# Standard products leave the recurrence over chunks; score and value products are regrouped

## Time and profile before

| what | value |
|---|---|
| median of three runs | 2170.67 us (2167.99 to 2173.81) |
| the profiled execution's own time | 2169.13 us |
| its span, first to last instruction | 2167.2 us |
| TensorE busy, matmul / weight loads | 98% / 86% |
| VectorE / ScalarE / GpSimd busy | 49% / 19% / 23% |
| mean granted TensorE clock | 0.997 of full |
| L782, all standard products | 2816 records, 697.3 us |

### The profile page before, as it was taken

The page is one execution under the profiler, slowest core; times in us unless marked ns, Lnnn a source line. Parts: engine busy times, 40 slices in busy tenths (PEclk is TensorE's granted clock), DMA queues, the critical chain, the costliest instruction groups (busy, mean ns, idle before and its releaser), DMA issues.

```text
span 2167.2 us, 48810 instructions
## 1 busy us (share of the span) xinstructions
PE 2132.3 (98%) x21490; PEld 1869.5 (86%) x21490; DVE 1065.8 (49%) x1786; ACT 409.5 (19%) x1169; POOL 505.5 (23%) x377
## 2 busy tenths in 40 slices
PE   9999999999999999999999999999999999999997
PEld 8999977777887679999899999777778877799996
DVE  4554344442726624773645443444437265247745
ACT  1111122222103511110211121222221034111002
POOL 3433300002011123333224333000020111234331
PEclk9999999999999999999999999999999999999998
DMA  8544333335633365554354453222355333655551
GB/s 295 175 163 169 125 121 106 107 106 194 221 138 97 98 231 178 161 178 161 125 174 167 156 175 125 101 101 100 100 210 196 137 98 107 242 167 166 171 174 66
DMA packets 88979, 329.50 MB, mean 152 GB/s; under 512 B 11904, under 2 KB 11920, under 8 KB 86464
## 3 DMA queue, kind: packets, MB, share of 16 engines
q1 hardware_dynamic: 74592, 268.60, 36.8%
q0 software_dynamic: 11872, 53.59, 6.8%
q10 hardware_dynamic: 2304, 4.20, 0.6%
HBM read 315.91 MB, written 18.82 MB: 154 GB/s over the span
## 4 chain that ended last, share of the span: by engine, by line
PE 94%; DVE 2%; DMA 1%; ACT 1%; issue 0%; SPq 0%; POOL 0%; DVEq 0%; POOLq 0%
PE PB L782 29%; PE PB L832 3%; PE PB L850 3%; PE PB L846 3%; PE PB L841 3%; PE PB L836 3%; PE PB L823 3%; PE PB L826 3%; PE PB L1238 3%; DMA WT<-in_w_all 1%; PE PB L906 1%; PE PB L988 1%; PE PB L971 1%; PE PB L973 1%; PE PB L966 1%; PE PB L962 1%
## 5 line engine op out<-in xcount | busy, mean ns | idle before, releaser
L782 PE MATMUL PB<-XT,WT 128*128 128x264 f32 (+1 forms) x2816 | 697.3, 395 | 1.6 <-DMA WT<-in_w_all 1.6
L782 PEld LDWEIGHTS PB<-XT,WT 128*128 128x128 f32 (+1 forms) x2816 | 506.0, 189 | 107.1 <-issue 19.6
L1433 ACT ACTIVATE VT<-PB 128x132 f32<-128x132 f32 (+2 forms) x280 | 79.1, 291 | 580.1 <-PE PB L836 131.4
L617 POOL DMA_DIRECT2D out<-in_c_win x16 | 8.1, 506 | 471.2 <-DVE ARENA L1998 471.2
L1433 ACT ACTIVATE ARENA<-PB 128x128 f32<-128x128 f32 (+6 forms) x173 | 73.1, 447 | 223.8 <-PE PB L762 56.9
L617 POOL DMA_DIRECT2D ARENA<-in_c_sel x64 | 40.0, 625 | 238.5 <-issue 238.5
L638 POOL TENSOR_TENSOR TOEP<-WT 128x1024 f32<-128x1024 f32 x20 | 47.2, 2358 | 181.3 <-PE PB L836 133.8
L638 POOL TENSOR_TENSOR TOEP<-H 128x1024 f32<-128x1024 f32 x20 | 48.2, 2409 | 139.9 <-PE PB L836 135.4
L832 PE MATMUL PB<-ARENA,TOEP 128*128 128x132 f32 x640 | 78.7, 276 | 0.5 <-POOL TOEP L641 0.5
L836 PE MATMUL PB<-ARENA,TOEP 128*128 128x132 f32 x640 | 78.6, 276 | 0.0
L841 PE MATMUL PB<-ARENA,TOEP 128*128 128x132 f32 x640 | 78.6, 276 | 0.0
(11 more groups left out here) (450 smaller groups left out, 4177.5 us busy)
## 6 DMA issues: line engine op xcount, KB each, us to landing
WT<-in_w_all SPq DMA_DIRECT2D x340, 512.0 KB, 4.5
H<-in_w_all SPq DMA_DIRECT2D x120, 512.0 KB, 4.5
KNVC<-in_w_all SPq DMA_DIRECT2D x40, 512.0 KB, 3.9
out<-in_c_win POOLq DMA_DIRECT2D x16, 512.0 KB, 4.9
ARENA<-in_c_cmp POOLq DMA_DIRECT2D x64, 128.0 KB, 5.0
ARENA<-in_c_sel POOLq DMA_DIRECT2D x64, 128.0 KB, 4.8
TOEP<-in_toep POOLq DMA_DIRECT2D x2, 2048.0 KB, 8.4
ARENA<-in_states POOLq DMA_DIRECT2D x4, 1024.0 KB, 11.5
```

The lines of the kernel that those rows point to most:

```text
L782: ins = mm(PB[rows, bank, 0:T], WT[:, s, k, 0:rows.stop - rows.start], x, start=start, stop=stop)
L1433: return act(out, in_, ACT.Copy)
```

## The change

1. In the recurrence no standard product is issued behind `r`, `u` and the result products (`BEHIND` 0 in place of 1); `EARLY` falls from 21 to 18. The 48 products a layer that this frees are issued in front of the gate pairs (90 in place of 42). All other counts of the plan stay.
2. The four result products with the old state move from behind `s` to behind `r`; in front of them TensorE waits for ScalarE's copy of the chunk before (`o`).
3. A unit's score products are reordered: 256, 512, 512, then the wait, then 256.
4. The compressed values are made by 48 products with 32 weight columns, in turn for the four column groups, and lie on all 128 partitions: the samples' in bank 1 (two for each column group), the prompt's in bank 2. VectorE takes them out with two instructions over 128 partitions.
5. The samples' attention follows: the transposed compressed scores are made at four places, ScalarE copies `PCZ` in four parts for each parity, the products with compressed values use rows 32m to 32m + 14 for column group m, and the products with the new rows come first, with a step `n` that the compressed ones wait for.

```diff
-EARLY = 21
+EARLY = 18
...
-    BEHIND.update({f"r{chunk}": 1, f"u{chunk}": 1, f"s{chunk}": 1})
+    BEHIND.update({f"r{chunk}": 0, f"u{chunk}": 0, f"s{chunk}": 0})
...
                         mark("rw_t", it, ins, f"r{c}")
+                        if c:
+                            wait(("rw_a", f"o{c - 1}"))
+                        for w, cq in pairs:
+                            for ra in both:
+                                mm(PB[ra, 2, cq], ST[ra, c % 2, w, :], AR[ra, w * NCH + c, 1, :], start=False, stop=True, skip_group_check=True)
                         project(L, hq, f"r{c}")
...
                         mark("rw_t", it, ins, f"s{c}")
-                        for w, cq in pairs:
-                            for ra in both:
-                                mm(PB[ra, 2, cq], ST[ra, c % 2, w, :], AR[ra, w * NCH + c, 1, :], start=False, stop=True, skip_group_check=True)
...
-                        for s in range(NSQ):
-                            for g in range(NG):
-                                ins = mm(PB[0:NBLK, 1 + s // 2, (s % 2) * 256 + g * HD:(s % 2) * 256 + g * HD + HD],
-                                         hx[:, g // 2, s, g % 2, :], W2[:, :], start=True, stop=True)
-                    if kd:
-                        for r in range(4):
-                            for g in range(NG):
-                                ins = mm(PB[32 * r:32 * r + NBLK, 5, 256 + g * HD:256 + g * HD + HD],
-                                         hx[:, g // 2, NB, g % 2, :], W2[:, :], start=True, stop=True)
+                        blocks = lambda g, s: ARENA[:, at_hx + 135 * g + NBLK * s:at_hx + 135 * g + NBLK * s + 32]
+                        for g in range(NG):
+                            for i in range(2):
+                                for r in range(4):
+                                    ins = mm(PB[32 * r:32 * r + 32, 1, i * 256 + g * HD:i * 256 + g * HD + HD], blocks(g, 2 * r + i), W2[:, :], start=True, stop=True)
+                            for r in range(4):
+                                ins = mm(PB[32 * r:32 * r + 32, 2, g * HD:g * HD + HD], blocks(g, NB), W2[:, :], start=True, stop=True)
...
-                    for e in range(2):
-                        if e:
-                            pe.wait_ge(*step("sc_t", it, "s0"))
-                        ins = mm(PB[:, 2, e * 256:e * 256 + 256], H[half(e), Q0 + u, 0:P], keys(e)[:, :, 0:P], start=True, stop=True)
-                        if e == 0:
-                            mark("sc_t", it, ins, "s0")
-                        ins = mm(PB[:, 1 - e, :], H[half(1 - e), Q0 + u, P:SEQ], keys(1 - e)[:, :, 0:SEQ], start=True, stop=True)
+                    ins = mm(PB[:, 2, 0:256], H[half(0), Q0 + u, first], keys(0, P), start=True, stop=True)
+                    mark("sc_t", it, ins, "s0")
+                    mm(PB[:, 1, :], H[half(1), Q0 + u, second], keys(1, SEQ), start=True, stop=True)
+                    ins = mm(PB[:, 0, :], H[half(0), Q0 + u, second], keys(0, SEQ), start=True, stop=True)
+                    mark("sc_t", it, ins, "s1")
+                    pe.wait_ge(*step("sc_t", it, "s0"))
+                    ins = mm(PB[:, 2, 256:512], H[half(1), Q0 + u, first], keys(1, P), start=True, stop=True)
...
-                mark("as_t", L, transpose(PB[0:NBLK, 5, 0:P], SCS[:, 0:NBLK]), "pt")
+                for r in range(4):
+                    ins = mm(PB[32 * r:32 * r + NBLK, 5, 0:P], SCS[:, 0:NBLK], ident, start=True, stop=True)
+                mark("as_t", L, ins, "pt")
...
+                for br in range(2):
+                    for m in range(NB // 2):
+                        ins = mm(PB[32 * m:32 * m + 32, 4, 0:256], PNT[:, br, 32 * m:32 * m + 32],
+                                 VT[0:NB, 2, 2 * br * P:2 * br * P + 256], start=br == 0, stop=False)
+                mark("as_t", L, ins, "n")
...
+                    pe.wait_ge(*step("as_t", L, "n"))
                     for m in range(NB // 2):
                         b = 2 * m + odd
-                        mm(PB[32 * m:32 * m + 32, 4, 0:256], PCZ[:, b, :], VC[:, b, :], start=False, stop=False)
+                        rows = slice(32 * m, 32 * m + NBLK)
+                        ins = mm(PB[32 * m:32 * m + 32, 4, 0:256], PCZ[rows, b, :], VC[rows, odd, :], start=False, stop=odd == 1)
...
-                    copy(PCZ[:, odd:NB:2, cols], own_rows(PB[0:NBLK, 5, 0:P]))
+                    for m in range(NB // 2):
+                        rows = slice(32 * m, 32 * m + NBLK)
+                        copy(PCZ[rows, 2 * m + odd, cols], own_rows(PB[rows, 5, 0:P])[:, m])
...
-                        for r in range(4):
-                            rows = slice(32 * r, 32 * r + NBLK)
-                            stt(VCP[rows, :].rearrange("p (g d) -> p g d", d=HD), PB[rows, 5, 256:512].rearrange("p (g d) -> p g d", d=HD),
-                                0.5, spread(B2V[rows, L, :].unsqueeze(1), NBLK, NG, HD), ALU.mult, ALU.add)
-                        src = PB[0:NBLK, 1:6, :].rearrange("p a b -> p (a b)")[:, 0:NSQ * 256].rearrange("p (g d) -> p g d", d=HD)
-                        ins = stt(KNVC[0:NBLK, :].rearrange("p (g d) -> p g d", d=HD), src, 0.5,
-                                  spread(B2V[0:NBLK, L, :].unsqueeze(1), NBLK, NSQ * NG, HD), ALU.mult, ALU.add)
+                        stt(VCP.rearrange("p (g d) -> p g d", d=HD), PB[:, 2, 0:256].rearrange("p (g d) -> p g d", d=HD),
+                            0.5, spread(B2V[:, L, :].unsqueeze(1), P, NG, HD), ALU.mult, ALU.add)
+                        ins = stt(KNVC[:, 0:8 * HD].rearrange("p (g d) -> p g d", d=HD), PB[:, 1, :].rearrange("p (g d) -> p g d", d=HD), 0.5,
+                                  spread(B2V[:, L, :].unsqueeze(1), P, 2 * NG, HD), ALU.mult, ALU.add)
```

More of the change, by code:

```diff
@@ L208, in hybrid_trunk @@
         KN = KNVC[:, 0:8 * T].rearrange("p (t n) -> p t n", n=T)
-        VC = KNVC[0:NBLK, :].rearrange("p (s n) -> p s n", n=4 * HD)
+        VC = KNVC[:, 0:8 * HD].rearrange("p (i n) -> p i n", n=4 * HD)
         V1 = sb("V1", [P, 8, 32])
@@ L290, in hybrid_trunk @@
         used[0] -= 9 * T
+        at_hx = used[0]
         HX, HY, HT = take(P, 2, 270), take(P, 2, 270), take(P, 2, 270)
@@ L312, in hybrid_trunk @@
         PTZ = take(P, 4 * NB, 32).rearrange("p (i b) n -> p i b n", b=NB)
-        PCZ, PNT, OS = take(NBLK, NB, 32), take(NB, 2, P), take(P, 256)
+        PCZ, PNT, OS = take(P, NB, 32), take(NB, 2, P), take(P, 256)
         assert used[0] <= at_att
@@ L379, in hybrid_trunk @@
         steps("cb", DEPTH, t="sc pt", v="zero add max sub sum rc cg ok ps", a="exp pt")
-        steps("sc", DEPTH * UNITS, t="s0 s", v="add max", a="exp")
+        steps("sc", DEPTH * UNITS, t="s0 s1 s", v="add max", a="exp")
         steps("pv", DEPTH * UNITS, t="pt0 pt1 o", v="rc cg ps", a="pt0 pt1")
         steps("po", DEPTH * UNITS, v="o")
-        steps("as", DEPTH, t="sc0 sc1 pt o tr", a="exp pt os", v="zero q gm gsr add max rc cg ps back")
+        steps("as", DEPTH, t="sc0 sc1 pt n o tr", a="exp pt os", v="zero q gm gsr add max rc cg ps back")
         steps("zb", DEPTH, a="tanh", v="sz out")
@@ L1277, in scores @@
                     it = L * UNITS + u
-                    keys = lambda a: H[half(a), KV0 + 4 + g2:KV0 + 9 + g2:4]
-                    for e in range(2):
-                        if e:
-                            pe.wait_ge(*step("sc_t", it, "s0"))
-                        ins = mm(PB[:, 2, e * 256:e * 256 + 256], H[half(e), Q0 + u, 0:P], keys(e)[:, :, 0:P], start=True, stop=True)
-                        if e == 0:
-                            mark("sc_t", it, ins, "s0")
-                        ins = mm(PB[:, 1 - e, :], H[half(1 - e), Q0 + u, P:SEQ], keys(1 - e)[:, :, 0:SEQ], start=True, stop=True)
+                    keys = lambda a, n: H[half(a), KV0 + 4 + g2:KV0 + 9 + g2:4][:, :, 0:n]
+                    first, second = slice(0, P), slice(P, SEQ)
+                    ins = mm(PB[:, 2, 0:256], H[half(0), Q0 + u, first], keys(0, P), start=True, stop=True)
[5 more added lines that the diff above has]
+                    ins = mm(PB[:, 2, 256:512], H[half(1), Q0 + u, first], keys(1, P), start=True, stop=True)
                     mark("sc_t", it, ins, "s")
@@ L1369, in _ @@
                             mm(PB[32 * m:32 * m + 32, 4, 0:256], PTZ[:, i, 2 * m + odd, :], SVS[odd][:, m, i, :],
-                               start=odd == 0 and i == 0, stop=False)
+                               start=False, stop=False)
+                    pe.wait_ge(*step("as_t", L, "n"))
                     for m in range(NB // 2):
                         b = 2 * m + odd
-                        mm(PB[32 * m:32 * m + 32, 4, 0:256], PCZ[:, b, :], VC[:, b, :], start=False, stop=False)
-                for br in range(2):
-                    for m in range(NB // 2):
-                        ins = mm(PB[32 * m:32 * m + 32, 4, 0:256], PNT[:, br, 32 * m:32 * m + 32],
```

(3 more changed lines are left out.)

## The result

| | before | changed |
|---|---|---|
| median of the runs, us | 2171.38 (2167.99 to 2173.81, 4 runs) | 2195.2 (2191.39 to 2206.61, 4 runs) |
| ratio, 95% interval | 1 | 1.0124 (1.0103 to 1.0146) |
| profiled execution and its span, us | 2169.13, 2167.2 | 2191.39, 2189.7 |
| mean granted clock, each run | 0.997 (profiled) | 0.983, 0.987, 0.987, 0.989 |

The change makes the kernel slower by 1.2%, about 24 us. The forecast was 2176.4, its range 2170.5 to 2188.0: the time lies outside. The last line of the table holds the main cause.

A forecast was written before the change was run, and what follows sets the result against it. TensorE was taken as the bound, at 94% of the chain that ended last. Recurrence and moved products net +15.2, values -7.4, scores -4.1, sample attention +2.0: +5.7, so 2176.4 us against the median, range 2170.5 to 2188.

The forecast's parts named there:

- the fourth rival: Recurrence chunks: the clock falls once they lose their filling, +22 us more, 2198; chance 0.03.
- The recurrence's static saving: Recurrence: shorter pauses take a chunk from 3.52 to 2.66 us; over 32 chunks -27.5 us.
- The 96 moved products: Run ahead of the gates: standard products taken from the chunks cost 0.445 us each there, +42.7 us.
- Compressed values: Compressed values: four column groups stream side by side, 1.6 us in place of 5.29; -7.4 us in all.
- Scores: Score products: a unit takes 1.48 in place of 1.82 us; twelve units count, -4.1 us.
- Sample attention: Sample attention: six more copies, a change of product kind and three more products cost 1.0 us, twice: +2.0 us.
- The new waits: Waits for o in the chunks and for step n in the sample attention: passed under other work, cost nothing.
- The first rival: Recurrence: pauses don't shrink, 0.24 us is the true hand-over, a chunk of 3.23 us, 2194.6; chance 0.09.
- the second: Values and scores: packing fails, column groups and row halves run one after the other, 2187.9 us; chance 0.07.
- The sum without the recurrence: Forecast terms of values (-7.4), scores (-4.1) and sample attention (+2.0) together: -9.5 us.

The follow-up runs named there:

- e5: Changed kernel with useless filler products in the chunks' pauses, 128 columns behind r, 256 behind u and s: 2185.38 us, ratio 1.0072.
- e7: Changed kernel with the first half of the result products back behind s: 2205.07 us, ratio 1.0164.
- e2: Changed kernel with the recurrence's part undone, so all of the change but that: 2163.81 us, ratio 0.9959 against before.
- e1: Kernel before with the recurrence's part of the change alone: 2207.63 us, ratio 1.0168.
- e9: Kernel before with the new order of the scores alone: 2167.12 us, ratio 0.9977.
- e6: Kernel with all but the recurrence's part, plus six standard products of each layer moved in front of two waits: 2156.62 us, ratio 0.9927 against before.

## Why the prediction was wrong

**The step that failed is the clock's.** The forecast held it at 1.00 in the chunks and gave its fall, the fourth rival, 0.03, with the words that a chunk "would have products streaming in 1.15 of 2.66 us, and its longest gap is below 0.6". The argument took the one row with a level below 1.00, at 2.96 busy of 17 us, as if nothing between that and full work could lower it. The earlier trace rows said nothing of the range between. And its sentence that the trace shows a lower level "only at the end" is wrong. The trace of before has these windows in layer 1, ahead of a round's chunks, the first with an idle time of 1.56 us near its end:

```profile
1456.00:1459.70 3.70, 2.14 (x37) 1.58 (x38) 0.69 (x1) 0.17 (x1) 0.00 (x0) 1.00 0.03 10
1459.70:1463.10 3.40, 3.40 (x38) 2.39 (x38) 0.69 (x2) 0.22 (x1) 0.00 (x0) 0.50 0.02 5
```

So a short pause amid small products had been followed by the low level before anything was changed. Windows over the whole span, and not over three stretches, would have found it. The runs then showed more: with 7.31 us busy of 10.80 in the chunks the clock fell in four of eight rounds, in e5, with 10.4 of 10.8, in the chunks of none. The rival's price per chunk was right (0.72 measured, 0.69 forecast). Its extent was not: it took all 32 chunks, +22; in the profiled run seven or eight were hit, some in part, which cost 3 us (first r to last s takes 11.07, 10.41, 10.04 and 10.16 in the four rounds, 9.68 in the others). The rest lies in the work behind them, whose standard products stream twice as long. In all that is 7 us in the two profiled executions (against e5), and 11 to 20 by the ratios of the changed kernel (1.0124, 1.0145) and e7 (1.0164) against e5's 1.0072.

The Trainium skill, "TensorE: Matmul & The Clock Gate", A second HAM failure mode, reports a kernel whose clock swung because TensorE idled briefly and often. The traces agree: idle times of 0.35 to 0.38 in each chunk, and stretches of 7 to 10 us at the low level. The prediction named this rule and set it aside for want of a row, though its own trace had one, the two windows above.

**The recurrence's static saving** was -27.5. The chunk is right within 0.02. But e5, at a full clock, saves 24.8 against the profiled execution of before, and 673.02 - 651.37 = 21.7 against e2, which differs only in this part and the fillers. What is missing is about 1 us of a low stretch at 1570 to 1573, 0.1 in each round, where the work behind the last chunk (L1052) now waits for ScalarE, and time that the profile calls issue, in which TensorE waits for nothing that it shows: 9.1 us in e5, 5.2 in e2. It is 5.8 in the changed kernel, 7.1 in e1 and 9.5 in e7, against 5.7 in before. Whether empty chunks cause it stays open.

**The 96 moved products** were +42.7. Measured 40.22 - 18.86 = 21.36 in each layer: right.

**Compressed values** were -7.4, measured -3.81 twice, -7.6: right. Four column groups do stream side by side, with 48 products in 1.48.

**Scores** were -4.1. A unit gains 0.33 as forecast (0.34), and the wait on VectorE grows by 0.3. e9 measures -0.23% (-0.10 to -0.35), 5 us, which agrees.

**Sample attention** was +2.0, measured +1.47 twice, +2.9, inside its bounds. The mis-sized term is the copies': 17 take 2.70 and not 2.2, 0.159 each where 0.128 was read, so 0.84 of waiting remained and not 0.5 to 0.6.

**The new waits**, for o in front of the moved half and for step n, cost nothing, as forecast. The first rival (pauses don't shrink) falls by the chunk of 2.68, the second (packing fails) by the values' 1.48. That the first rival's 2194.6 is close to the measured 2195.2 is luck: its chunk of 3.23 isn't there.

**The sum without the recurrence** was -9.5; e2 measures -0.41% (-0.23 to -0.59), 8.9 us. What remains above the forecast once the clock is kept in the rounds, e5's 15.6 us of span against +5.7, can be read from the stage table: the rounds saved 2.7 less, the run from the compressed scores to the gates took 5.9 more, the stage from the gates to the next rounds 1.2 more. Of the 5.9, some 1.7 are the sample attention's and the longer wait on VectorE. The other 4.2 go with the low stretches there, four of 3.4 us in e5 and none in the profile of before; that they cost all of it is an estimate, since only the known terms were taken off. What the 1.2 is stays open.

## What to carry to other kernels

A filler product has a price and two returns. Here three standard products in a chunk cost 0.84 us, but gave back their own 1.34, and held the clock, which was worth another 11 to 20 us in each run. Before a loop with short waits is emptied, ask what TensorE's busy time per round becomes, and if it falls well below anything that the trace shows at a full clock, treat the clock as open and not as safe. The mean clocks of a few runs show it: here 0.979 to 0.989 against 0.993 to 0.998 in the kernels with three products in a chunk. And look at the clock over the whole span of the kernel before, in short windows: its 3.4 us at the low level were there to be seen.

And waits that a regrouping leaves (1.8 and 0.84 us here) can be filled with products from a long run elsewhere: e6 is 0.7% faster than before.

## What was not expected of the hardware

The granted clock fell to its lower level inside chunks in which TensorE never idled for longer than 0.4 us at a time, and stayed there for 7 to 10 us. The set of rounds was another in each of two executions of the same program, and the same kernel ran between 2191.39 and 2206.61 us.

Fillers that used only two of the four 64 by 64 blocks of the array, 0.2 to 0.4 us in each pause, were enough to keep it at 1.00 in the chunks of e5's profiled execution.

Low stretches of 3 to 7 us also lay at the compressed scores or behind the wait on VectorE that follows them, in one layer or both, in every profiled run but that of before, whether the rounds were full or not. A stage with 6.8 us of them took about 2 to 3 us longer than its other terms give (e2 and e5), one with 3.4 about 1 us.
